# Expert gate and up matrices loaded whole and multiplied one after the other, down rows side by side

## The reference

```python
def swiglu(x, w_gate, w_up, w_down):
    return (jax.nn.silu(x @ w_gate) * (x @ w_up)) @ w_down
# 64 experts, each token goes to 8 of them with gates g:
y = swiglu(ht[tok], w_gate[e], w_up[e], w_down[e])   # w_gate, w_up: 1024 x 256; w_down: 256 x 1024
acc = acc.at[tok].add(g[:, None] * y)
```

## Time and profile before

| | |
|---|---|
| median of 3 runs | 1457.09 us (1451.98 to 1457.18) |
| the profiled execution | 1455.79 us, its span 1454.0 us |
| mean granted TensorE clock | 0.958 |
| busy: PE, DVE, ACT, POOL | 1308.9, 470.9, 250.0, 159.8 us |
| moved | 496.12 MB, 341 GB/s over the span |

### The profile page before, as it was taken

The page is one execution under the profiler, slowest core; times in us unless marked ns, Lnnn a source line. Parts: engine busy times, 40 slices in busy tenths (PEclk is TensorE's granted clock), DMA queues, the critical chain, the costliest instruction groups (busy, mean ns, idle before and its releaser), DMA issues.

```text
span 1454.0 us, 23748 instructions
## 1 busy us (share of the span) xinstructions
PE 1308.9 (90%) x6741; PEld 646.2 (44%) x6741; DVE 470.9 (32%) x1109; ACT 250.0 (17%) x516; POOL 159.8 (11%) x590
## 2 busy tenths in 40 slices
PE   3999999999999999796789999999999999969764
PEld 0464644444444444342347474444444444424331
DVE  1523632233222322221562462322223222222125
ACT  0133211111111111110212221111111111111011
POOL 0000021111111111110000002101111111111010
PEclk8989999999999999998899999999999999989887
DMA  9985769999999999999997666295999999999992
GB/s 349 384 332 179 299 243 388 374 402 368 391 381 377 387 381 389 409 399 402 363 410 275 235 229 245 95 386 198 389 378 397 365 391 361 396 391 409 398 410 96
DMA packets 130561, 496.12 MB, mean 341 GB/s; under 512 B 16168, under 2 KB 16176, under 8 KB 123840
## 3 DMA queue, kind: packets, MB, share of 16 engines
q1 hardware_dynamic: 130496, 495.17, 88.8%
HBM read 494.04 MB, written 1.08 MB: 341 GB/s over the span
## 4 chain that ended last, share of the span: by engine, by line
PE 78%; DVE 8%; issue 6%; DMA 3%; SPq 2%; ACT 1%; DVEq 0%; POOL 0%; ACTq 0%; POOLq 0%
PE ps L839 30%; PE ps L855 15%; PE ps L876 7%; PE ps L772 6%; PE ps L782 4%; PE ps L705 4%; DMA ring<-in_w_ada 3%; DVE temp L1170 2%; PE ps L848 2%; PE ps L728 1%; PE ps L640 1%; DVE w L1395 1%; PE ps L808 1%; PE ps L788 1%; ACT w L1016 1%
## 5 line engine op out<-in xcount | busy, mean ns | idle before, releaser
L839 PE MATMUL ps<-ring,w 128*64 128x512 f32 (+1 forms) x2432 | 434.5, 610 | 71.0 <-issue 67.8
L839 PEld LDWEIGHTS ps<-ring,w 128*64 128x64 f32 (+1 forms) x2432 | 148.9, 128 | 327.3 <-issue 327.0
L855 PE MATMUL ps<-ring,w 128*32 128x512 f32 (+1 forms) x1216 | 219.0, 597 | 0.0
L1395 DVE SCALAR_TENSOR_TENSOR w<-ps,w 128x256 f32<-128x256 f32 x60 | 29.0, 484 | 471.2 <-ACT w L1016 471.2
L772 PE MATMUL ps<-hx,scat 128*128 128x512 f32 x496 | 146.7, 418 | 0.9 <-issue 0.9
L1383 DVE CAST scat<-ps 128x512 fp32r<-128x512 f32 x120 | 83.0, 692 | 167.4 <-PE ps L855 167.4
L876 PE MATMUL ps<-scat 128*128 128x512 f32 x480 | 125.5, 403 | 0.0
L1016 ACT ACTIVATE w<-ps 128x256 f32<-128x256 f32 x60 | 23.1, 384 | 567.7 <-PE ps L839 567.7
L1078 POOL CAST idg<-G 128x4 fp32r (+1 forms) x256 | 40.1, 187 | 650.9 <-PE ps L788 635.7
L772 PEld LDWEIGHTS ps<-hx,scat 128*128 128x128 f32 x496 | 83.9, 189 | 61.4 <-issue 50.3
L855 PEld LDWEIGHTS ps<-ring,w 128*32 128x32 f32 (+1 forms) x1216 | 61.6, 125 | 108.6 <-issue 104.1
(11 more groups left out here) (220 smaller groups left out, 898.0 us busy)
## 6 DMA issues: line engine op xcount, KB each, us to landing
ring<-in_w_exp_gate SPq DMA_DIRECT2D x256, 512.0 KB, 8.1
ring<-in_w_exp_up SPq DMA_DIRECT2D x256, 512.0 KB, 9.4
ring<-in_w_exp_down SPq DMA_DIRECT2D x128, 1024.0 KB, 10.8
ring<-in_w_ada SPq DMA_DIRECT2D x48, 1024.0 KB, 8.6
w<-in_w_out SPq DMA_DIRECT2D x2, 4096.0 KB, 21.5
w<-in_w_in SPq DMA_DIRECT2D x2, 2400.0 KB, 17.9
w<-in_w_uq SPq DMA_DIRECT2D x2, 1728.0 KB, 12.5
ring<-in_w_ukv SPq DMA_DIRECT2D x2, 1536.0 KB, 15.8
```

Source lines behind the costliest of these rows:

```text
L839: last = mm(ps[unit * g:unit * g + unit, B_F, :].rearrange("p (q f) -> p q f", q=2), hTb[:, kt, unit * g:unit * g + unit], gate_up(k)[:, : ...
L855: last = mm(ps[unit * g:unit * g + unit, bank, :], midT[:, f, unit * g:unit * g + unit], down_w(k)[:, f, half * 512:(half + 1) * 512], sta ...
L1395: v.scalar_tensor_tensor(mid, ps[:, B_F, F:2 * F], gslot, sil, ALU.mult, ALU.mult).then_inc(s["mid_ready"], 1)
```

## The change

In the transfers, the first step of a refill loads the gate matrices whole (1 MB, 8 KB in a row per partition) when `gate_done` is raised, and the second step the up matrices whole. The down matrix is laid with `(p k)`: a partition gets rows 2p and 2p+1, which lie side by side in HBM, 8 KB in one piece. In the block, TensorE makes the whole gate product into bank `B_F` in matmuls of 256 columns, raises `gate_done`, and then makes the whole up product into bank `B_1`. ACT takes silu after `gate_done`; DVE also waits for `gu_done` and reads up from `B_1`. The transposes take every second column of the middle, to match the rows of down.

```diff
             def load_gate_up(l, half, slots, experts):
-                kts = slice(half * KT // 2, (half + 1) * KT // 2)
+                dst, w = ((gate_w, w_exp_gate), (up_w, w_exp_up))[half]
                 for slot, e in zip(slots, experts):
-                    for dst, w in ((gate_w, w_exp_gate), (up_w, w_exp_up)):
-                        src = w[ds(l, 1), ds(e, 1)].rearrange("a b (p k) f -> p (a b k) f", k=KT)
-                        sp.dma_start(dst(slot)[:, kts, :], src[:, kts, :]).then_inc(gu_landed[half][slot // 2], 16)
+                    src = w[ds(l, 1), ds(e, 1)].rearrange("a b (p k) f -> p (a b k) f", k=KT)
+                    sp.dma_start(dst(slot), src).then_inc(gu_landed[half][slot // 2], 16)
             def load_down(l, slots, experts):
-                    sp.dma_start(down_w(slot), w_exp_down[...].rearrange("a b (k p) d -> p (a b k) d", p=P))
+                    sp.dma_start(down_w(slot), w_exp_down[...].rearrange("a b (p k) d -> p (a b k) d", k=FT))
...
-                    sp.wait_ge(s["gu_half_done"], used)
+                    sp.wait_ge(s["gate_done"], used)
...
-                            for kt in range(KT):
-                                if kt == KT // 2:
-                                    last.then_inc(s["gu_half_done"], 1)
-                                    for q in halves:
-                                        pe.wait_ge(gu_landed[1][q], loads * 64)
-                                    passed(pe)
-                                for g, k in enumerate(slots):
-                                    last = mm(ps[unit * g:unit * g + unit, B_F, :].rearrange("p (q f) -> p q f", q=2),
-                                              hTb[:, kt, unit * g:unit * g + unit], gate_up(k)[:, :, kt, :],
-                                              start=kt == 0, stop=kt == KT - 1)
+                            def project(weights, bank):
+                                for kt in range(KT):
+                                    for g, k in enumerate(slots):
+                                        last = mm(ps[unit * g:unit * g + unit, bank, 0:F], hTb[:, kt, unit * g:unit * g + unit],
+                                                  weights(k)[:, kt, :], start=kt == 0, stop=kt == KT - 1)
+                                return last
+                            project(gate_w, B_F).then_inc(s["gate_done"], 1)
+                            for q in halves:
+                                pe.wait_ge(gu_landed[1][q], loads * 32)
+                            passed(pe)
+                            last = project(up_w, B_1)
                             last.then_inc(s["gu_done"], 1)
...
-                                last = tr(ps[:, B_T, f * P:(f + 1) * P], mid[:, f * P:(f + 1) * P], ident)
+                                last = tr(ps[:, B_T, f * P:(f + 1) * P], mid.rearrange("p (q k) -> p k q", k=FT)[:, f, :], ident)
...
-                        act.wait_ge(s["gu_done"], b + 1)
+                        act.wait_ge(s["gate_done"], b + 1)
...
                         dve.wait_ge(s["sil_ready"], b + 1)
+                        dve.wait_ge(s["gu_done"], b + 1)
...
-                        v.scalar_tensor_tensor(mid, ps[:, B_F, F:2 * F], gslot, sil, ALU.mult, ALU.mult)
+                        v.scalar_tensor_tensor(mid, ps[:, B_1, 0:F], gslot, sil, ALU.mult, ALU.mult)
```

More of the change, by code:

```diff
@@ L196, in down_w @@
             return ring[:, s * SLOT_W + 2 * KT * F:(s + 1) * SLOT_W].rearrange("p (k d) -> p k d", k=FT)
-        def gate_up(s):
-            return ring[:, s * SLOT_W:s * SLOT_W + 2 * KT * F].rearrange("p (q k f) -> p q k f", q=2, k=KT)
         ada = [ring[:, s * ADA_W:(s + 1) * ADA_W].rearrange("p (g n) -> p g n", g=4) for s in range(ADA_BUFS)]
@@ L336, in decoder_trunk @@
         shsil_ready shmid_ready sel_ready sh_gate_done rank_done table_ready rg_ready
-        sh_landed gu_half_done S_ready gath_done hT_ready gu_done sil_ready mid_ready midT_done midT_ready down_done
+        sh_landed gate_done S_ready gath_done hT_ready gu_done sil_ready mid_ready midT_done midT_ready down_done
         ST_done ST_ready y0_ready y1_ready scat_done sh_free out_done ang_ready hi_ready y_free count_ready key_ready place_ready order_done gc_ready rc_ready pro_link
@@ L407, in load_gate_up @@
             def load_gate_up(l, half, slots, experts):
-                kts = slice(half * KT // 2, (half + 1) * KT // 2)
+                dst, w = ((gate_w, w_exp_gate), (up_w, w_exp_up))[half]
                 for slot, e in zip(slots, experts):
-                    for dst, w in ((gate_w, w_exp_gate), (up_w, w_exp_up)):
-                        src = w[ds(l, 1), ds(e, 1)].rearrange("a b (p k) f -> p (a b k) f", k=KT)
-                        sp.dma_start(dst(slot)[:, kts, :], src[:, kts, :]).then_inc(gu_landed[half][slot // 2], 16)
+                    src = w[ds(l, 1), ds(e, 1)].rearrange("a b (p k) f -> p (a b k) f", k=KT)
+                    sp.dma_start(dst(slot), src).then_inc(gu_landed[half][slot // 2], 16)
             def load_down(l, slots, experts):
                 for slot, e in zip(slots, experts):
-                    sp.dma_start(down_w(slot), w_exp_down[ds(l, 1), ds(e, 1)].rearrange("a b (k p) d -> p (a b k) d", p=P)).then_inc(down_landed[slot // 2], 16)
+                    sp.dma_start(down_w(slot), w_exp_down[ds(l, 1), ds(e, 1)].rearrange("a b (p k) d -> p (a b k) d", k=FT)).then_inc(down_landed[slot // 2], 16)
             def row(dst, src, sm_):
@@ L527, in _ @@
             tr = nc.tensor.transpose
-            start_counts(pe, "gu_half_done gu_done midT_done ST_done scat_done", "gath_done gT_done down_done",
+            start_counts(pe, "gate_done gu_done midT_done ST_done scat_done", "gath_done gT_done down_done",
                          [s["sh_free"], *ada_used])
@@ L824, in _ @@
                         for q in halves:
-                            pe.wait_ge(gu_landed[0][q], loads * 64)
+                            pe.wait_ge(gu_landed[0][q], loads * 32)
                         passed(pe)
@@ L1394, in _ @@
                         passed(dve)
-                        v.scalar_tensor_tensor(mid, ps[:, B_F, F:2 * F], gslot, sil, ALU.mult, ALU.mult).then_inc(s["mid_ready"], 1)
+                        v.scalar_tensor_tensor(mid, ps[:, B_1, 0:F], gslot, sil, ALU.mult, ALU.mult).then_inc(s["mid_ready"], 1)
                         dve.wait_ge(s["midT_done"], b + 1)
```

## The result

The changed kernel took 1436.0 us (median of 4 runs, 1434.12 to 1438.13) against 1456.3 for the kernel before: ratio 0.9867, 95% interval [0.9842, 0.9891]. Once more beside the experiments it was 0.9855 [0.9837, 0.9874]. The forecast was 1437. The profiled execution's span went from 1454.0 to 1434.2 us.

| stretch | before, us | after, us | difference |
|---|---|---|---|
| first layer, from the first block to the quad before the waiting quads | 361.1 | 356.6 | -4.5 |
| second layer, the same | 347.5 | 339.9 | -7.6 |
| the five cycles with three blocks | 310.3 | 304.2 | -6.1 |
| all else | 435.1 | 433.5 | -1.6 |

A forecast was written before the change was run, and what follows sets the result against it. TensorE was taken to pace 45 of 60 blocks and transfers the five three-block cycles (310.3 us). From 1455.8 us, 7.2 for TensorE, 10.2 for transfers and 1.0 for two stops gave 1437, range 1429 to 1453.

The forecast's parts named there:

- TensorE's term: 45 TensorE-paced blocks: 0.21 us saved by the early silu less 0.05 for narrower matmuls, 7.2 us in all.
- 0.21 us: Between first gather and transposes: TensorE's wait for the middle in each block, removed by running silu beside the up product.
- the two stops inside L839: Waits for the refill's second step in the middle of two blocks' products; faster loads shorten them, 1 us for both.
- The transfers' term: Five three-block cycles, paced by transfers: 8 KB pieces raise 410 GB/s to 424, saving 3.3%, 10.2 us.
- of 310.3 us that is 10.2: The 3.3% rate saving applied to the whole 310.3 us of the five three-block cycles.
- (a): Rival, expert transfers: longer pieces bring nothing, 424 GB/s having come from w_ada's layout or quieter engines; 1448 us, chance 0.16.
- (b): Rival, L839 in quads: TensorE can't take load-matmul pairs every 0.054 us; 1541 us, mild form 1451; chance 0.06 each.
- (c): Rival, round starts: the longer program is fetched late, 0.74 us more in each of 48 rounds; 1473 us, chance 0.05.
- (d): Rival, more gain: TensorE-paced cycles lose both stops and stretches at the border gain too; about 1427 us, chance 0.05.

The follow-up runs named there:

- c1: The changed kernel itself, with no edit, run and profiled a second time on one chip beside other runs: 1435.0 us, ratio 0.9855.
- e10: Changed kernel plus ten idle matmuls before the weight wait of the five waiting quads, repeated on the same chip as c1: 1432.3 us, ratio 0.9837.
- e8: Kernel before the change plus eleven idle matmuls ahead of the same five waiting quads: 1450.9 us, ratio 0.9988.
- e1: Changed kernel with its expert weights (gate, up and down) in pieces of 4 KB again: 1446.7 us, ratio 0.9942.
- e6: Changed kernel with gate and up products in matmuls of 128 columns, twice as many matmuls and weight loads: 1479.5 us, ratio 1.0189.
- e5: Changed kernel plus ten idle matmuls before the weight wait of the five waiting quads, first run: 1432.2 us, ratio 0.9855.

## Why the prediction was right, and where its terms were not

**The time and its sign** came out as forecast: 1437 foreseen, 1436.0 measured. That the number is so close is luck: two errors of 4 us of opposite sign cancel.

**TensorE's term was undersized.** The mechanism held, the size did not. "0.21 us" for the silu off the path is 0.20 in the quad read and 0.23 in the median (1.27 to 1.04); the row was from the first layer, and in the second the wait was longer. Missing was the distance from the transposes to the second gather, 0.19 to 0.145 us: their weight loads now run under the first gather. The prediction names this cover and counts no gain for it. The product costs 0.04 us more, not 0.05. Together 0.24 a block, not 0.16 (the median period of a block in the four-block stretches fell from 16.29 to 16.05). The prediction counts 45 blocks; two of them, the quads at the layers' ends, wait 11.06 and 10.84 us for weights, and 43 are left: x 0.24 = 10.3; the two stops inside L839, 0.97 and 1.54 us, both went, and a new one of 0.45 came: 2.1, where "1 us for both" was counted, and the working given for it (10 us of transfers x 3.3%) makes only 0.3 for each. Sum 12.4, measured 12.2.

**The transfers' term was mis-sized for the time, not for the rate.** "424 GB/s is what pieces of 8 KB have been seen to reach" held: 422. The step that failed is "of 310.3 us that is 10.2", which measured 6.1 (7.6 in c1): it took the five cycles as transfers at their ceiling throughout. They were not, before or after. Length times rate in the rows makes 124.4 MB for the five cycles of either kernel; at 410 GB/s that takes 303.5 us, at 422 it takes 294.8, so 8.7 us is what the rate alone could save. The rest of the cycles is time in which the transfers ran below their ceiling: 6.8 us before, 9.4 after (7.2 in c1).

By cycle, the two that begin without a wait gave 4.4 us (122.4 to 118.0), and 3.3% of them is 4.0. The three that begin with a waiting quad gave 1.7 us of 187.9 (3.6 in c1), where 6.2 were foreseen. At the start of such a cycle the ring is full and only TensorE frees it, at the lower clock. The gates are refilled 5.5 to 6.6 us after the quad's start in the kernel before, 6.2 to 6.8 in the changed one and 5.8 to 6.1 in c1. Faster transfers meanwhile finish their queue earlier. In the changed kernel's first profile the refill came 2.6 and 2.7 us before the last queued landing at two of these quads, and the next matrices took 3.8 and 4.0 us to land behind it. At the third quad and in c1, with 3.2 to 3.5 us, they took 2.5, which is the full rate. Those 2.8 us are more than the 1.5 by which this profile lies over c1. And c1, without them, is still 2.6 us short of the forecast.

Released at 3.9 us, in e10, the cycles take 300.4 us. But e8 wins 2.8 in the kernel before in the same way, and in both the time below the ceiling falls to about 4 us. So the clock costs both kernels, and the pieces' gain stays at 7.1 us when it is taken away. What else holds the cycles below the ceiling stays open. One candidate is in SP's rows: the quad that starts at 612.28 frees the gate slots 2 and 3 with the same product as 0 and 1, but SP, which goes through the slots in order, refills them only at 631.45, after the down matrices of slots 0 and 1 at 628.52. No run changed that order.

The rule of about 3 cycles per packet in the Trainium skill ("DMA: Bandwidth & Descriptors", section "Why small descriptors are slow (HBM only)") gave 1.1%; the trace has 422 against 410 GB/s, 2.9%, and the measurement decides.

**The pieces also work where the forecast gave them nothing.** e1 shows 11 us for them in all, about half outside the three-block cycles, and most of that half in one quad of its profile. In the kernel before, the second step landed 0.1 to 1.4 us ahead of its need in ten of the eleven quads that don't wait at their start; with faster blocks and the old pieces TensorE runs into it, as e1 shows. The forecast took TensorE's gain and the transfers' gain as belonging to different cycles.

**Rivals.** (a) fell with e1. (b) fell at 0.054 us a pair, and e6 saw 0.028. (c) did not occur at the place it named: after a quad the gap is 0.74 us as before. Inside a quad it seems to have cost c1 and e5 one stop each, of about 1 us idle, and e6 far more. (d) happened in part.

## What to carry to other kernels

A profile that shows one engine setting the pace and transfers at 384 of 410 GB/s is a balance of two: shortening one side uses up the other's margin, so measure for each wait how early its data lands, not only whether it waits. A faster transfer in a ring is worth its rate only as long as slots are free; look at when the consumer releases them and in which order they are refilled. Before you blame a cause for a shortfall, take it away in the kernel before as well: keeping TensorE warm looked like the missing 4 us until e8 won 2.8 of them without the change. And profile the same kernel twice. Here the transposes with a stride cost nothing as long as their weight load ran ahead; without that cover they cost 0.07 us a block.

## What the runs showed of the hardware

- Expert loads in pieces of 8 KB moved 422 GB/s and in pieces of 4 KB 410, with the queue never empty.
- Loading weights for a 128-column transpose took 140 ns from adjacent float32 columns and 198 ns from every second column.
- In four column tiles of 32, TensorE took a weight load and a 128-column matmul every 0.028 us for 98 pairs in a row (204 in the longest run), and then stopped for 0.6 to 3.3 us without a wait in the program. The 14 such stops of e6 (one of them in a pair block) ended 2.2 to 2.6 us after the start of a packet of the instruction queue.
- TensorE came out of a shorter idle time no faster: after 9.50 us idle the quad's product began at the lower clock level, 1.2 GHz, and took 10.01 us; after 11.41 us idle in the kernel before it took 8.98 us, and after 10.15 us in c1_changed 8.99 us.
- Kept busy through the wait (e10), the same quad's gate half took 3.66 us and the granted clock of the cycle was 1.00. In e5 the clock fell at two quads all the same, behind 2.65 and 2.05 us of idle time.
